# Two chained transformer blocks with routed experts: the order in which expert weights and first rows reach TensorE

## The chip, the cores and the metric

The kernel runs on one core of one Trainium2 chip. The metric is the device time of one execution in microseconds (us). Before the change the median of three runs is 1183.91 us (1180.22 to 1186.23).

## What is computed

Two transformer blocks follow each other on 256 tokens of width 1024, all in float32. The first has pooling and sparse attention, cross attention to a memory, and a mixture of 32 experts; the second has two attentions and a mixture of 64 experts with a shared one. The change touches only the two mixtures. Cut to what matters, the reference of an expert layer is:

```python
# first block: h has 256 rows, 32 experts, the best two of one group of eight
out = out + jnp.einsum('nef,efd->nd', silu(h @ w_gate[e]) * (h @ w_up[e]) * gates[e], w_down[e])
# second block: 64 experts, the best eight of four groups, weights summing to 2.5
g = jnp.sum(one_hot(eidx, 64) * w[..., None], axis=-2)
routed = sum over e of (silu(h @ w_eg[e]) * (h @ w_eu[e]) * g[:, e, None]) @ w_ed[e]
return routed + (silu(h @ w_sg) * (h @ w_su)) @ w_sd
```

An expert takes 1024 inputs to 256 hidden values and back, so its weights are 6 MB: 2 MB each of gate, up and down. The host packs them per expert into `w1_pack` and `w2_pack`, 128 partitions by 6144 columns: columns 0 to 2047 are gate and up for the first four chunks of the inputs (k = 0 to 3), columns 2048 to 4095 those for k = 4 to 7, and columns 4096 to 6143 are the down weights, ordered by output half (1024 columns for outputs 0 to 511, then 1024 for 512 to 1023).

## The kernel before

**Quads.** Only the rows that chose an expert are computed with it. They come in slabs of at most 32 rows, and four slabs make a quad: they stand in the four 32-wide lanes of one 128-row tile, each lane with its own expert. For one quad all four experts' weights are needed, 12 MB in each part of three: part g = 0 (k = 0 to 3, four lanes of 1024 KB), g = 1 (k = 4 to 7) and g = 2 (down), 4 MB a part. They live in `quad_w`, a view of the buffer `wring` by part and lane. Each part has one buffer, so it is loaded again when the quad before has used it. All weights are loaded by SP (SyncE) on one queue, in program order: for quad i it waits for `quad_gate_up_half` and loads part 0 for the next, for `quad_gate_up_made` and loads part 1, for `quad_down_made` and loads part 2 (L586 to L611 in the first block, L616 to L650 in the second). `load_lane` (L491) is one DMA of 1024 KB for a lane of part 0 or 1. `load_down` (L487) is one DMA of 512 KB for one output half of a lane; the callers issue half 1 of all four lanes and then half 0 of all four, and each half has its own semaphore.

PE (TensorE) does a quad in `quad` (L1041): the matmuls of part 0 and part 1 (L1066), eight transposes of the next quad's rows (`turn_rows`, L1037), two of the hidden values (L1077), then the down matmuls of half 1 (L1088), a mixing matmul that adds them to their tokens (L1097), and the same for half 0. It waits for the weights of a half by that half's semaphore:

```python
for half in (1, 0):
    ...
    pe.wait_ge(E(f"moe{n}_quad_down_loaded{half}"), i * 64)
```

The first block has eight quads. The first two are written out, with weights for the second in buffers that are free then (`second_gate_up`, `second_half`); only its parts of 1 for lanes 2 and 3 and its down weights go into `wring`. The rest is a loop over a register.

**Large items.** In the second block experts with more than 32 rows are done first, as tiles of up to 128 rows, two per pass of a loop (`items` of each engine). SP loads such an item's gate and up weights (2048 KB, L515) once PE has used the buffer, and its down weights (1024 KB, L525). Between the passes 1 and 2 (counted from 0) SP also loads parts of the first quad: `first_half` (L551) is part 1 for lanes 0 and 1, into `kmT_vm` and `tmp`. Lanes 2 and 3 of part 1 are loaded when the last item has freed `wring`. After the items come the quads; for this input there are five, and they gather the items' results meanwhile.

DVE (VectorE) prepares the first item: after the lists are made it runs `tile_shares` (L1986 to L2008: gate values per row, then the one-hot tiles for the quads' gates and the rows of the results), `quads_opened`, and then the scaling of the first item's rows out of PSUM (L2209), for which PE waits. POOL (GpSimd) gathers rows and stores results through its own DMA queue.

## Time and profile before

| | |
|---|---|
| Median of three runs | 1183.91 us |
| The profiled execution's own time | 1184.56 us |
| Its span in the trace | 1182.7 us |
| PE busy (matmul) | 991.0 us, 84% |
| DVE / ACT / POOL busy | 413.3 / 204.6 / 179.2 us |
| DMA moved | 382.71 MB, 324 GB/s on average |
| Mean granted PE clock | 0.925 of full |

The busy share of PE is an average over stages. The projections and attentions are PE's, with the DMA engines partly idle; the quads have the DMA engines full and PE waiting. So the table says where time is spent, and the chain of waits and the windows by stage say what each stage is bound by. The execution's own time is 1.86 us more than its span.

### The profile page before, as it was taken

The page shows a single profiled execution, that of the slowest core. Times are in us where ns is not written, and L with a number is a line of the kernel's source. Part 1 is how long each engine was busy: PE and PEld are TensorE (multiplying, and loading weights), DVE is VectorE, ACT ScalarE, POOL GpSimd, SP SyncE. Part 2 cuts the span into 40 slices and gives each one's busy share as a digit, 9 for nine tenths or more (in the row PEclk, how much of TensorE's full clock was granted, in tenths as well). Part 3 has the DMA queues.
Part 4 walks back from the last instruction along what each step waited for, and adds up shares of the span by engine and source line. Part 5 has one row for each costly group of instructions (what it writes and reads, how often), then busy time and mean ns, then how long its engine had stood idle before and what let it go on. Part 6 is the DMA issues. An engine that isn't in the chain of part 4 may idle for free.

```text
span 1182.7 us, 13815 instructions
## 1 busy us (share of the span) xinstructions
PE 991.0 (84%) x4939; PEld 531.1 (45%) x4939; DVE 413.3 (35%) x929; ACT 204.6 (17%) x439; POOL 179.2 (15%) x242
## 2 busy tenths in 40 slices
PE   6999998895786666689999998879999999965666
PEld 3545533342221111134556545468688787611111
DVE  1795212235100000024754123764323333145412
ACT  2204201311110101130533303101111111100000
POOL 1000010100000000000000000054455454133000
PEclk9999998896988878899999998889999999997788
DMA  8551567897989999973469886789999999999996
GB/s 316 209 213 72 197 243 314 305 365 307 407 345 417 417 417 416 419 235 130 170 257 343 327 334 246 322 330 417 364 358 362 367 363 351 356 414 416 414 417 274
DMA packets 79841, 382.71 MB, mean 324 GB/s; under 512 B 22008, under 2 KB 24308, under 8 KB 54523
## 3 DMA queue, kind: packets, MB, share of 16 engines
q1 hardware_dynamic: 64075, 330.64, 72.0%
q0 software_dynamic: 15728, 51.58, 11.5%
q8 instruction: 22, 0.36, 0.1%
q14 instruction: 16, 0.13, 0.0%
HBM read 347.05 MB, written 50.24 MB: 336 GB/s over the span
## 4 chain that ended last, share of the span: by engine, by line
PE 47%; DMA 21%; DVE 3%; SPq 2%; issue 1%; ACT 1%; DVEq 0%; POOLq 0%
DMA wring<-in_w_pack 21%; PE bank L887 16%; PE bank L1133 13%; PE bank L1145 6%; PE bank L1066 6%; PE bank L1088 1%; SPq L493 1%; PE bank L898 1%; PE bank L1097 1%; PE bank L952 1%; PE bank L919 1%; PE bank L1037 0%; SPq L489 0%; DMA kT<-xn_dram,token_now 0%; PE bank L926 0%
## 5 line engine op out<-in xcount | busy, mean ns | idle before, releaser
L887 PE MATMUL bank<-wring,hT 128*128 128x512 f32 (+3 forms) x608 | 249.7, 571 | 5.7 <-DVEq L1714 3.8
L1066 PE MATMUL bank<-wring,kT 128*32 128x512 f32 x768 | 118.1, 753 | 74.8 <-DMA wring<-in_w_pack 72.1
L887 PEld LDWEIGHTS bank<-wring,hT 128*128 128x128 f32 x608 | 114.0, 200 | 132.4 <-issue 122.5
L1133 PE MATMUL bank<-qT,wring 128*128 128x128 f32 x1408 | 163.0, 279 | 8.2 <-DVE qT L2209 5.6
L1133 PEld LDWEIGHTS bank<-qT,wring 128*128 128x128 f32 x1408 | 162.5, 196 | 13.1 <-DVE qT L2209 5.9
L1066 PEld LDWEIGHTS bank<-wring,kT 128*32 128x32 f32 x768 | 28.0, 134 | 157.5 <-DMA wring<-in_w_pack 88.3
L760 POOL DMA_INDIRECT PRT<-xn_parts_dram,part_now x88 | 89.7, 1019 | 40.0 <-issue 29.8
L1145 PE MATMUL bank<-wring,PRT 128*128 128x512 f32 x176 | 77.4, 592 | 0.0
L1097 PE MATMUL bank<-yT 128*128 128x512 f32 x104 | 55.2, 655 | 19.6 <-ACT yT L1534 5.7
L887 PE MATMUL bank<-wring,yT 128*128 128x512 f32 x160 | 71.0, 597 | 0.7 <-ACT yT L1440 0.7
L1088 PE MATMUL bank<-wring,kiT 128*32 128x512 f32 x416 | 55.4, 654 | 11.0 <-ACT kiT L1529 5.7
L2149 DVE TENSOR_TENSOR PRT<-bank,PRT 128x256 f32<-128x256 f32 x13 | 5.5, 423 | 163.5 <-ACT PRT L1527 163.5
L2231 DVE TENSOR_TENSOR PRT<-bank,PRT 128x256 f32<-128x256 f32 x22 | 9.3, 425 | 129.7 <-ACT PRT L1513 129.7
L1145 PEld LDWEIGHTS bank<-wring,PRT 128*128 128x128 f32 x176 | 32.6, 190 | 36.8 <-issue 36.8
L1440 ACT ACTIVATE wring<-bank 128x512 f32<-128x512 f32 (+3 forms) x40 | 21.8, 563 | 157.8 <-PE bank L887 156.1
L2221 DVE TENSOR_SCALAR qT<-yT,gs,modc 128x128 f32<-128x128 f32 x176 | 47.9, 347 | 0.8
L1527 ACT ACTIVATE PRT<-bank 128x256 f32<-128x256 f32 x13 | 5.0, 384 | 248.4 <-PE bank L1066 248.4
L887 PEld LDWEIGHTS bank<-wring,yT 128*128 128x128 f32 x160 | 29.7, 190 | 40.1 <-issue 39.0
L1097 PEld LDWEIGHTS bank<-yT 128*128 128x128 f32 x104 | 18.6, 199 | 59.1 <-ACT yT L1532 13.8
L734 POOL DMA_DIRECT2D wring<-in_w_ada x24 | 12.8, 532 | 211.7 <-PE bank L1179 73.5
L808 POOL COPY token_now<-token_list 128x1 uint32 (+1 forms) x15 | 4.0, 269 | 252.4 <-PE bank L1037 218.8
L855 POOL COPY kmT_vm<-tmp 128x1024 f32<-128x1024 f32 x2 | 2.1, 1040 | 255.4 <-DVEq L1714 255.4
(372 smaller groups left out, 1028.7 us busy)
## 6 DMA issues: line engine op xcount, KB each, us to landing
wring<-in_w_pack SPq DMA_DIRECT2D x118, 1024.0 KB, 16.5
wring<-in_w_pack SPq DMA_DIRECT2D x104, 512.0 KB, 17.8
wring<-in_w_pack SPq DMA_DIRECT2D x22, 2048.0 KB, 9.4
y_dram<-gateB SPq DMA_DIRECT2D x8, 4096.0 KB, 19.4
wring<-in_w_ada POOLq DMA_DIRECT2D x24, 1024.0 KB, 6.7
wring<-in_pack_z.0 SPq DMA_DIRECT2D x1, 2048.0 KB, 10.9
wring<-in_pack_z.2 SPq DMA_DIRECT2D x1, 2048.0 KB, 17.2
wring<-in_pack_z.3 SPq DMA_DIRECT2D x1, 2048.0 KB, 8.8
```

What stands on the lines that cost most here:

```text
L493: sp.dma_start(quad_w[:, g, j, :], A[f"w{n}_pack"][bass.ds(e, 1), :, 2048 * g:2048 * (g + 1)].rearrange("o p n -> p (o n)"))\
L734: pool.dma_start(w, A["w_ada_2"][0][k * P:(k + 1) * P, cols_]).then_inc(E(f"ada_loaded{q % ADA_BUFFERS}"), 16)
L760: pool.indirect_dma_start(xg[:, slot, 256 * g:256 * (g + 1)], None, xn_parts_dram, bass.IndirectOffsetOnAxis(ap=part_now[:, slot, g:g + 1] ...
L887: mm = nc.tensor.matmul(b[:, 0:n], lhs(k, t), w[:, k, c0:c0 + n], start=(k == 0), stop=(k == nk - 1))
L898: tr = nc.tensor.transpose(b[0:m, j * P:(j + 1) * P], piece, ident[:])
L1066: mm = nc.tensor.matmul(bank[lane[j], 0, :], xqT[:, k, lane[j]], w[:, (k % 4) * 512:(k % 4 + 1) * 512], start=(k == 0), stop=(k == KD - 1))
L1088: mm = nc.tensor.matmul(bank[lane[j], 2 + half, :], hidqT[:, f, lane[j]], quad_w[:, 2, j, c0:c0 + 512], start=(f == 0), stop=(f == 1))
L1097: mm = nc.tensor.matmul(bank[:, 4 + 2 * t + half, :], mix[:, t * P:(t + 1) * P], ysq[:, half, :], start=first, stop=False, skip_group_chec ...
L1133: mm = nc.tensor.matmul(bank[:, 2 + s, f * P:(f + 1) * P], item_gate_up(s)[:, k, f * P:(f + 1) * P], xT[:, s, k, :], start=(k == 0), stop= ...
L1145: mm = nc.tensor.matmul(bank[:, 4 * s + half, :], hidT[:, s, f, :], item_down(s)[:, half, f, :], start=(f == 0), stop=(f == 1))
L1440: drained(nc.scalar.activation(dst, src, func, scale=scale))
L2221: ins = V.tensor_scalar(xT[:, slot, k, :].rearrange("p (g w) -> p g w", g=4), blocks[:, k], gain[:, k:k + 1], shift[:, k:k + 1], ALU.mult, ...
```

## The change

- **First item's rows early.** `tile_shares` is cut in two. The first part (gate values) stays; the one-hot tiles and the result rows become `gate_tiles`, which DVE runs after the first pass of items. `quads_opened(2)` comes before `tile_shares`.
- **Whole down weights.** `load_down` loads a lane's down weights in one DMA of 1024 KB, with one semaphore for both halves, and PE waits for all four lanes before half 1. This holds for every quad but the last of each block.
- **Last four slabs in pieces.** The last quad of each block leaves the loop. SP loads its part 1 and part 2 by `load_last`, as pieces of 512 KB: k = 4, 5 of all lanes, then k = 6, 7, then down half 1, then half 0, each piece with its own semaphore. PE turns the next rows between part 0 and part 1 and waits in the middle of part 1. A third entry of `pairs_n` holds the number of the quad before the last, read into registers by PE and SP.
- **A third half lane.** Part 1 for lane 2 of the second block's first quad is loaded with the two others among the first large items, into `gateB[:, 0, :]` and `qiT`, as two DMAs of 512 KB. After the items SP loads the second quad's part 1 for lane 2 in its place.

The core of the diff:

```diff
-            def load_down(n, half, j, e):
-                c0 = 1024 * half
-                sp.dma_start(quad_w[:, 2, j, c0:c0 + 1024], A[f"w{n}_pack"][bass.ds(e, 1), :, 4096 + c0:5120 + c0].rearrange("o p n -> p (o n)"))\
-                    .then_inc(E(f"moe{n}_quad_down_loaded{half}"), 16)
+            def load_down(n, j, e):
+                sp.dma_start(quad_w[:, 2, j, :], A[f"w{n}_pack"][bass.ds(e, 1), :, 4096:6144].rearrange("o p n -> p (o n)"))\
+                    .then_inc(E(f"moe{n}_quad_down_loaded"), 16)
+
+            def load_last(n, g, experts):
+
+                for part in ((0, 1) if g == 1 else (1, 0)):
+                    c0 = 1024 * part
+                    for j, e in enumerate(experts):
+                        sp.dma_start(quad_w[:, g, j, c0:c0 + 1024], A[f"w{n}_pack"][bass.ds(e, 1), :, 2048 * g + c0:2048 * g + c0 + 1024].rearrange("o p n -> p (o n)"))\
+                            .then_inc(E(f"moe{n}_last_loaded{2 * g + part}"), 16)
...
-                for j in range(2):
+                for j in range(3):
                     e = sp.value_load(item_base[0:1, j:j + 1], min_val=0, max_val=E2 - 1)
-                    load_first_half(j, first_half[j], e)
+                    if j < 2:
+                        load_first_half(j, first_half[j], e)
+                    else:
+                        for part in range(2):
+                            sp.dma_start(third_half[part], A["w2_pack"][bass.ds(e, 1), :, 2048 + 1024 * part:3072 + 1024 * part].rearrange("o p n -> p (o n)"))\
+                                .then_inc(E("moe2_first_half_loaded"), 16)
...
-                with sp.Fori(3, quads_n) as i:
+                before_last = last_quad(sp, 1)
+                with sp.Fori(3, before_last) as i:
...
+                load_part(0, before_last, experts)
+                for g in (1, 2):
+                    sp.wait_ge(E(freed[g]), before_last)
+                    load_last(1, g, experts)
...
-                for j in (2, 3):
-                    load_first_half(j, quad_w[:, 1, j, :], first[j])
+                load_lane(2, 1, 2, second[2])
+                load_first_half(3, quad_w[:, 1, 3, :], first[3])
...
-                load_quad(1, second, (range(4), (2, 3)))
+                load_quad(1, second, (range(4), (3,)))
...
+                        if g == 1 and last is not None:
+                            pe.wait_ge(E(f"moe{n}_quad_result_copied"), i)
+                            turn_rows(i * 16 + 16)
...
+                        elif g == 1 and last is not None:
+                            pe.wait_ge(E(f"moe{n}_last_loaded2"), 64)
...
+                            if k == 6 and last is not None:
+                                pe.wait_ge(E(f"moe{n}_last_loaded3"), 64)
...
-                        pe.wait_ge(E(f"moe{n}_quad_down_loaded{half}"), i * 64)
+                        if last is not None:
+                            pe.wait_ge(E(f"moe{n}_last_loaded{4 + half}"), 64)
+                        else:
+                            pe.wait_ge(E(f"moe{n}_quad_down_loaded"), i * 64)
...
                 pairs = pair_count(dve)
+                quads_opened(2)
+
                 tile_shares()
-                quads_opened(2)
...
                 pair_of(0)
+                gate_tiles()
                 gates_taken()
```

The order of DVE at the first item. Before (`kT` and `share` are the gate values, `kmT_vm` and `y_rows` the one-hot tiles and result rows, `qT<-bank` the rows that PE waits for):

```order
L1995 TENSOR_REDUCE share<-kT 128x16
L1996 TENSOR_SCALAR st<-st 128x16
L2000 TENSOR_TENSOR kmT_vm<-lists,st 128x136
L2001 TENSOR_TENSOR kmT_vm<-kmT_vm,share 128x136
L2000 TENSOR_TENSOR kmT_vm<-lists,st 128x136
L2001 TENSOR_TENSOR kmT_vm<-kmT_vm,share 128x136
L2004 TENSOR_SCALAR st<-st 128x16
L2005 TENSOR_TENSOR share<-share,st 128x16
L2006 TENSOR_TENSOR st<-st 128x16
L2007 TENSOR_SCALAR st<-st 128x16
L2008 TENSOR_TENSOR y_rows<-st 128x16
L2209 TENSOR_SCALAR qT<-bank,gs,modc 128x128 x8
```

With the change, at the same place:

```order
L2044 TENSOR_REDUCE share<-kT 128x16
L2264 TENSOR_SCALAR qT<-bank,gs,modc 128x128 x8
L2271 STREAM_TRANSPOSE yT<-PRT 128x1024
L2276 TENSOR_SCALAR qT<-yT,gs,modc 128x128 x8
L2286 TENSOR_TENSOR PRT<-bank,PRT 128x256
```

Ten instructions now stand behind the first pass of items, and the rows follow the reduction.

The order of SP in the first block, from the first quad's extra buffers to the loop. Before (`wring<-in_w_pack 128x1024` is a half of a lane's down weights, 128x2048 a whole lane of a part):

```order
L493 DMA wring<-in_w_pack 128x2048 x4
L598 DMA wring<-in_w_pack 128x2048 x2
L493 DMA wring<-in_w_pack 128x2048 x2
L489 DMA wring<-in_w_pack 128x1024 x8
L493 DMA wring<-in_w_pack 128x2048 x2
L489 DMA wring<-in_w_pack 128x1024 x8
L448 TENSOR_LOAD pairs_n
```

With the change:

```order
L506 DMA wring<-in_w_pack 128x2048 x4
L613 DMA wring<-in_w_pack 128x2048 x2
L506 DMA wring<-in_w_pack 128x2048 x2
L494 DMA wring<-in_w_pack 128x2048 x4
L506 DMA wring<-in_w_pack 128x2048 x2
L494 DMA wring<-in_w_pack 128x2048 x4
L449 TENSOR_LOAD pairs_n
L454 TENSOR_LOAD pairs_n
```

The bytes and their order by part are the same; eight half transfers have become four whole ones at both places, and a second register load follows.

The order of SP among the first large items, with the change (`kmT_vm` and `tmp` are the lanes 0 and 1 as before, `gateB` and `qiT` the added lane 2, and the 128x4096 transfer behind them is the next pass's first item):

```order
L568 DMA kmT_vm<-in_w_pack 128x2048
L556 TENSOR_LOAD item_base
L556 ISA x2
L568 ISA
L568 DMA tmp<-in_w_pack 128x2048
L556 TENSOR_LOAD item_base
L556 ISA x2
L561 ISA
L561 DMA gateB<-in_w_pack 128x1024
L561 ISA
L561 DMA qiT<-in_w_pack 128x1024
```

The two last transfers are new here; the loop over the passes follows them on the same queue.

## Rows read from the trace of the kernel before

**Rows 1.** The page, parts 2 and 4: rate per slice, shares of the chain

```profile
GB/s 316 209 213 72 197 243 314 305 365 307 407 345 417 417 417 416 419 235 130 170 257 343 327 334 246 322 330 417 364 358 362 367 363 351 356 414 416 414 417 274
...
PE 47%; DMA 21%; DVE 3%; SPq 2%; issue 1%; ACT 1%; DVEq 0%; POOLq 0%
```

**Rows 2.** Chain that ended last, second quad of the first block (start, us, what)

```profile
307.77 16.45 DMA wring<-in_w_pack
...
324.36 3.67 PE bank L1088 x16
...
332.49 2.27 PE bank L1088 x16
334.77 0.33 SPq L489
```

**Rows 3.** Windows there (length; busy time and instructions per engine; PE clock; DMA share; GB/s)

```profile
331.00:338.00 7.00, 6.27 (x30) 1.41 (x32) 0.40 (x2) 1.88 (x2) 0.00 (x0) 0.84 0.47 154
338.00:346.00 8.00, 7.82 (x70) 2.75 (x62) 1.32 (x4) 0.53 (x2) 0.19 (x1) 1.00 1.01 363
```

**Rows 4.** Windows in the first block, later: down weights, then gate and up weights

```profile
431.50:441.50 10.00, 8.02 (x44) 2.45 (x44) 1.26 (x3) 0.77 (x2) 0.18 (x1) 0.66 1.03 413
441.50:462.50 21.00, 11.38 (x72) 3.12 (x72) 1.23 (x4) 2.48 (x3) 1.02 (x1) 1.00 1.01 419
```

**Rows 5.** Timeline of PE, first block (start, us, what, idle before and its releaser)

```profile
370.68 5.34 PE L1066 MATMUL bank<-wring,kT 128*32 128x512 f32 x32 [4.75 <-DMA wring<-in_w_pack]
...
377.89 1.93 PE L1088 MATMUL bank<-wring,kiT 128*32 128x512 f32 x16 [0.47 <-ACT kiT L1529]
...
433.00 6.60 PE L1066 MATMUL bank<-wring,kT 128*32 128x512 f32 x32 [3.48 <-DMA wring<-in_w_pack]
...
453.90 3.64 PE L1066 MATMUL bank<-wring,kT 128*32 128x512 f32 x32 [3.23 <-DMA wring<-in_w_pack]
```

**Rows 6.** Chain, last quad of the first block

```profile
494.07 5.09 PE bank L1066 x32
...
505.67 1.90 PE bank L1088 x16
```

**Rows 7.** Chain, first large items of the second block

```profile
776.89 0.19 DVE st L1996
...
779.95 2.65 DVE qT L2209 x8
...
799.35 6.87 PE bank L1145 x16
...
818.61 15.68 DMA wring<-in_w_pack
```

**Rows 8.** Windows: first items; the other items; the quads after them

```profile
778.00:834.30 56.30, 49.13 (x328) 41.13 (x328) 25.73 (x74) 5.88 (x12) 26.92 (x36) 0.94 1.02 412
850.50:1019.80 169.30, 169.30 (x1154) 138.69 (x1153) 60.27 (x160) 23.53 (x48) 81.73 (x105) 1.00 0.95 358
1026.00:1160.00 134.00, 82.99 (x490) 24.64 (x488) 45.87 (x76) 4.16 (x10) 25.57 (x27) 0.82 1.02 412
```

**Rows 9.** Timeline: a result store of POOL, then the wait of PE

```profile
830.94 1.03 POOL L772 DMA_INDIRECT y_dram<-PRT,row_now  x1 [0.87 <-POOL row_now L767]
...
834.32 5.91 PE L1133 MATMUL bank<-qT,wring 128*128 128x128 f32 x36 [2.55 <-DMA wring<-in_w_pack]
```

**Rows 10.** Chain, last quad of the second block

```profile
1162.35 5.34 PE bank L1066 x32
...
1169.57 1.97 PE bank L1088 x16
...
1174.29 1.90 PE bank L1088 x16
```

**Rows 11.** Windows at the end of the last weights

```profile
1171.00:1172.00 1.00, 0.49 (x8) 0.00 (x0) 0.83 (x3) 0.00 (x0) 0.00 (x0) 1.00 0.12 49
1172.00:1173.00 1.00, 0.70 (x2) 0.46 (x3) 0.25 (x1) 0.00 (x0) 0.00 (x0) 1.00 0.00 0
```

More of the change, by code:

```diff
@@ L445, in quad_count, with last_quad @@
         def quad_count(engine, n):
-            least = FIXED_QUADS if n == 1 else 3
+            least = FIXED_QUADS if n == 1 else 4
             return engine.value_load(pairs_n[0:1, 1:2], min_val=least, max_val=QUADS[n])
+        def last_quad(engine, n):
+            least = FIXED_QUADS if n == 1 else 4
+            return engine.value_load(pairs_n[0:1, 2:3], min_val=least - 1, max_val=QUADS[n] - 1)
         def item_gate_up(s):
@@ L534, in items @@
                     if j >= 2:
-                        for half in (1, 0):
-                            load_down(2, half, j, e)
+                        load_down(2, j, e)
                 load_pair(1, True)
@@ L562, in first_quad @@
                 sp.wait_ge(E("ada_steps_made"), ADA_GROUPS * ADA_STEPS)
-                for half in (1, 0):
-                    for j in range(4):
-                        load_down(1, half, j, j)
+                for j in range(4):
+                    load_down(1, j, j)
                 sp.wait_ge(E("xn_ready"), 6)
@@ L586, in load_part @@
                     sp.wait_ge(E(freed[g]), made)
-                    for half in (1, 0) if g == 2 else (None,):
-                        for j in lanes:
-                            if g == 2:
-                                load_down(1, half, j, experts[j])
-                            else:
-                                load_lane(1, g, j, experts[j])
+                    for j in lanes:
+                        if g == 2:
+                            load_down(1, j, experts[j])
+                        else:
+                            load_lane(1, g, j, experts[j])
                 second, third = range(4, 8), range(8, 12)
@@ L624, in lane_after @@
                     else:
-                        for half in (1, 0):
-                            load_down(2, half, j, experts[j])
+                        load_down(2, j, experts[j])
                 first, second = quad_experts(0), quad_experts(1)
@@ L1038, in turn_rows, with quad @@
                     tr.then_inc(E(f"moe{n}_quad_rows_turned"), 1)
-                def quad(i, first):
-                    second = n == 1 and not first and isinstance(i, int)
+                def quad(i, first, last=None):
+                    second = n == 1 and not first and last is None and isinstance(i, int)
                     pe.wait_ge(E(f"moe{n}_quad_rows_copied"), i)
                     for g in range(2):
+                        if g == 1 and last is not None:
+                            pe.wait_ge(E(f"moe{n}_quad_result_copied"), i)
+                            turn_rows(i * 16 + 16)
                         if g == 0 and second:
@@ L1047, in quad @@
                         elif g == 0 and n == 1 and not first:
[L1048 removed]
+                            pe.wait_ge(E("moe1_quad_loaded0"), i * 64 - 64 if last is None else last * 64)
                         elif g == 1 and second:
@@ L1111, in quads @@
                 quads_n = quad_count(pe, n)
-                with pe.Fori(3 if n == 1 else 2, quads_n + 1) as i:
+                with pe.Fori(3 if n == 1 else 2, quads_n) as i:
                     quad(i, False)
+                quad(quads_n, False, last_quad(pe, n))
             def items():
@@ L1995, in tile_shares, with gate_tiles @@
                 link(V.tensor_reduce(share, same, X, ALU.add))
+            def gate_tiles():
+                k_n, q_n = TAKES[2], QUADS[2] + 1
+                row, item = [st[:, c:c + 16].rearrange("p (t k) -> p t k", t=2) for c in (326, 342)]
                 link(V.tensor_scalar(item, item, float(WHOLE), None, ALU.subtract))
@@ L2090, in quad_experts @@
                 link(V.tensor_scalar(whole, whole, float(FIXED_QUADS), None, ALU.add))
+                V.tensor_scalar(pairs_n[0:1, 2:3], whole, 1.0, None, ALU.subtract)
                 link(V.tensor_copy(pairs_n[0:1, 1:2], whole))
```

45 lines of the change are left out of this document (32 added, 13 removed).

## The prediction

> **What bounds the kernel now.** I read the page first for the rate of the DMA engines per slice and the shares of the chain [rows 1]. In three stretches the rate stands at 414 to 419 GB/s: slices 13 to 17, 36 to 39 and one around slice 28. 21% of the chain is the expert weights' DMA. So the quads of both blocks are bound by bytes, and there a change of order moves the end only if it changes the bytes in the stretch, lets the queue run dry, or changes what PE does behind the last transfer. Next I read windows by stage [rows 8]: the first items (778 to 834 us) run at 412 GB/s with a DMA share of 1.02, full too; the other items at 358 GB/s with PE busy all the time, so PE bounds them; the quads after them at 412 GB/s, full. Then the chain, for what each stretch waits on, and the timeline for PE within a quad.
>
> The transfers land in the order of their issue. A window of 10 us behind a part 1's landing moves at 413 GB/s and the 21 us behind it at 419 [rows 4]: 10 us is a part's 4 MB, so the first holds the half down transfers (512 KB) and the second the whole lanes (1024 KB). At 416 GB/s 2 MB take 5.0 us and 1 MB 2.5 us. I use this as a ruler for landings.
>
> **Part by part.** Signs: plus is slower.
>
> *Whole down weights, second quad of the first block: +4.5.* PE starts half 1 at 324.36, released by a DMA issued at 307.77; that is half 1 of all four lanes [rows 2]. Half 0 lands 5.0 us behind it by the ruler. With whole lanes PE needs both, so it starts at 329.4. From there to the release of SP takes 10.4 us (324.36 to 334.77), with the matmuls of half 1 at the lower clock already (3.67 us there [rows 2], 1.93 in [rows 5]). SP issues the third quad's down weights only then, and the queue runs dry meanwhile: 154 GB/s between 331 and 338 [rows 3]. The 5.0 us add to that drought, and all that follows in this block is FIFO behind it. Against it: between 338 and 346 the rate is only 363 GB/s [rows 3], 1.0 us of 8 lost, which with four issues in place of eight may go. Ends: +5.5 and, if the dip goes and the restart is quicker, +3.4. I take 4.5.
>
> *Whole down weights elsewhere in the first block: -0.6.* In the later quads PE wants half 1 at 377.89 [rows 5], 7.2 us behind part 1's landing at 370.7, and the whole part lands 10.1 us behind it. So PE waits 2.9 us more per quad, but the queue then still holds 8 MB (20 us) of the next parts, so it does not run dry and the wait is hidden; its cover is that queue. The rate of 413 becomes 419 for 4 MB: 0.15 us a quad, five quads, 0.75 us; the last quad's part 1 in pieces gives 0.15 back. Bounds: 0 and -1.5.
>
> At this place the Trainium skill speaks. The row shows that halving a transfer costs 1.4% of its rate while the queue is full [rows 4]. The Trainium skill, page "DMA: Bandwidth & Descriptors", sections "Anatomy of one DMA" and "Bandwidth", says a DMA takes some 2.0 us and its bytes at 436 GB/s, and to batch to at least 1 MiB. By that, as an estimate, eight halves cost 8 us more than four wholes, and the sum would be some 45 us faster. The trace does not bear it out: transfers overlap.
>
> *The last quad of the first block in pieces: -1.5.* Part 1 lands at 494.07 (call it T), PE starts down half 0 at 505.67, T + 11.6 [rows 6]. With pieces only k = 6, 7 is left at T: 1.8 us at the full clock (half of 3.64), 3.4 at the lower (half of 6.6) [rows 5], then 1.9 us to half 1 as in [rows 10] (1162.35 + 5.34 to 1169.57). That would give T + 5.3 at the latest; half 1 lands at T + 5.0 and half 0 at T + 10.1. So the weights behind it take over, and half 0 starts at T + 10.1. Bounds 0 and -2.6. The turned rows were beside the hidden values' path before, so moving them gives nothing.
>
> *First rows early and the third half, among the first items: 0 and +2.5.* DVE's ten instructions take 776.89 to 779.95, 3.1 us, on the chain [rows 7]; PE could start 3.1 us earlier. But PE waits 2.55 us until 834.32 for a DMA issued at 818.61 [rows 7, 9], and the stretch before it is full [rows 8]. Bytes ahead of that transfer decide when it lands, not PE. So the 3.1 us become a longer wait: worth 0. The third half puts 1 MB ahead of the same transfer: +2.5. Behind it PE is the bound, with the engines at 358 of 412 GB/s, so this passes whole to the end. `gate_tiles` moves to behind the first pass, where PE does 6.9 us of down matmuls (from 799.35 [rows 7]) before it needs them; 3 us are hidden there. Ends: -3.1 if the early rows pay fully and the megabyte is hidden, up to +5.0 if the result stores of the second pass (two of 512 KB, the first issued at 830.94 [rows 9]), now 3 us earlier, all go ahead too. The Trainium skill, same page, section "Queues, rings and completion order", says each DMA engine takes turns between the queues; no row here shows the turns themselves.
>
> *The quads of the second block: -2.9.* The stretch from 1026 to 1160 is full [rows 8]. It has 1 MB less (lane 2's part 1 of the first quad): -2.5. Three and a half quads' down weights whole, less part 1 in pieces: -0.4. In the fourth quad PE waits some 3 us more for half 1, under the queue again.
>
> *The last quad of the second block: -1.9.* T is 1162.35; half 0 starts at 1174.29, T + 11.9 [rows 10]. The last bytes pass between 1171 and 1172 and none after [rows 11]: T + 10 with the landing. So half 0 starts 1.9 us earlier. Bounds 0 and -3.4.
>
> *Small ones: +0.2.* One DVE instruction on the path to the second lists. The added register loads of PE and SP lie in front of waits for DMA.
>
> **Sum.** 4.5 - 0.6 - 1.5 + 2.5 - 2.9 - 1.9 + 0.2 = +0.3. Against the profiled execution (1184.56: the span of 1182.7 and 1.86 around it) this is 1184.9. The median is 0.65 below that execution, so I predict **1184.2** for the median. About 0.5% (5.9 us) is what a measurement of this kernel can tell from no change.
>
> **The rivals.**
>
> *The early rows pay (chance 0.21).* If the stretch from 778 is not as full as its share says, the 3.1 us arrive and the megabyte is hidden. For: the share is of engines busy, not of bytes at the best rate, 412 of 419. Against: PE waits at its end for a transfer issued 15.7 us earlier. Time: 1184.2 - 2.5 - 3.1 = 1178.6. With the tails at their better ends it is below 1178.
>
> *The pieces do not pay (0.13).* The 16 DMA engines end out of step, and each piece is in only when the slowest is. If half 0 lands at T + 11.6 or later in both blocks, both tails give 0: 1184.2 + 3.4 = 1187.6, and 1190 with the larger toll among the items. For it: the share falls off over several us at the end.
>
> *PE's clock (0.09), slower.* The chip grants PE 1.2 instead of 2.4 GHz behind idle stretches: a part's 32 matmuls take 6.60 or 3.64 us [rows 5]. The whole down weights put a third wait into each quad. If that keeps the clock at the lower level throughout, a quad is 13.2 us for two parts, up to 3.8 for transposes and hidden values (twice the 1.9), 10.4 from half 1 to SP's release [rows 2] and 3.7 for the last mixing (it takes as long as half 1): 31.1 us. Its bytes take 31.2 (370.68 to 433.00 is two quads [rows 5]). From there each further us of waiting in a quad goes to the end. At 1 us in each of eight such quads, and with no gain in the tails, it is 1184.2 + 8 + 3.4 = 1195.6. Against: the queue holds 20 us.
>
> *The number of transfers counts (0.02).* If each DMA had its issue, 0.43 us, in series, four fewer in ten quads less eight more in two would give -14: 1170. The rate of 413 against 419 speaks against it.
>
> *The change does less than it says* is not a rival here: the printed orders show each move.
>
> **The numbers.** Forecast as summed: 0.55, its own range 1180.5 to 1188.5. The range over all cases, 1177.5 to 1190, leaves out the clock case, the transfer count and the faster end of the first rival, some 0.2. Over 0.5% faster (below 1178): 0.4 of the early rows' 0.21, 0.02 of the count, and 0.05 of the rest: 0.15. Over 0.5% slower: 0.09, a third of the pieces' 0.13, and 0.05 from the forecast with its upper ends: 0.18. Within: 0.67.
>
> **What would show each step.** Down half 1 of the first block's second quad starts near 329, and the windows behind it are dry for 5 us longer. Later quads keep their 31 us distance. In both last quads down half 0 starts 10 us behind the last piece of part 1. PE's first item starts 3 us earlier by the clock of its own stretch, and the wait of the third pass (number 2) grows from 2.5 us to 8. From its end to the start of the quads nothing changes; from there to the last weight there are 2.9 us less. A third pass without a longer wait, or a second quad's half 1 without its 5 us, would prove the sum wrong.

## The result, and the profile after

The changed kernel takes **1185.80 us** (median of 20 runs) against 1181.12 us of the kernel before beside it (20 runs). The ratio is 1.0038, 95% interval 1.0024 to 1.0052: 4.5 us slower (2.8 to 6.2). The ratio's centre is within 0.5% and the median inside the forecast range, but the sum had +0.3 us. The profiled execution took 1191.89 us, near the upper end of its runs, so stages are read below from more than one trace. One run of e2 below, of 3474.34 us, is left out of its median and ratio.

One size given above needs a correction: 6144 columns of float32 on 128 partitions are 3 MB, so an expert's weights are 3 MB, 1 MB each of gate, up and down, and a quad's 12 MB are its three parts of 4 MB together. The argument uses the 4 MB.

I cut each trace into three stages by PE's timeline. *Front* runs from down half 1 of block 1's first quad to down half 0 of its last, *middle* from there to the first quad of block 2, *quads* from there to the end of the span. Before they are 205.7, 522.3 and 154.8 us; after 207.1, 525.7 and 157.3.

**Front.** Windows of the changed kernel at the place of [rows 3] (length; busy time and instructions per engine; PE clock; DMA share; GB/s):

```profile
331.00:338.00 7.00, 6.29 (x24) 1.59 (x20) 0.00 (x0) 0.60 (x1) 0.00 (x0) 0.60 0.11 46
338.00:346.00 8.00, 7.28 (x56) 2.13 (x52) 0.77 (x3) 1.88 (x2) 0.00 (x0) 1.00 0.78 296
```

The queue is dry for longer, as forecast: 46 in place of 154 GB/s, then 296 in place of 363. Against 416 GB/s these 15 us lose 8.5 us of transfer; before they lost 5.4. SP issues the third quad's down weights at 338.77:

```profile
338.77 1.98 SPq L494 DMA_DIRECT2D wring<-in_w_pack  x4
```

[Rows 2] have 334.77 there. The end of block 1, PE's timeline (start, us, what, idle before and its releaser):

```profile
492.16 1.92 PE L1109 MATMUL bank<-wring,kT 128*32 128x512 f32 x16
495.71 1.92 PE L1109 MATMUL bank<-wring,kT 128*32 128x512 f32 x16 [1.63 <-DMA wring<-in_w_pack]
...
500.94 3.37 PE L1135 MATMUL bank<-wring,kiT 128*32 128x512 f32 x16 [1.90 <-DMA wring<-in_w_pack]
505.02 1.98 PE L1144 MATMUL bank<-yT 128*128 128x512 f32 x4 [0.71 <-ACT yT L1580]
506.94 1.92 PE L1135 MATMUL bank<-wring,kiT 128*32 128x512 f32 x16
```

T, the landing of the last piece of part 1, is 495.71 (494.07 in [rows 6]). Half 1 comes at T + 5.2 as forecast; half 0 at T + 11.2, where I had T + 10.1. There is no wait ahead of half 0: its last piece had landed at T + 10.2 (505.89, by its semaphore), and PE was still at work. Its down half 1 ran mostly at the lower clock (3.37 us in place of 1.92), and with the mixing matmuls behind it PE takes 6.0 us from half 1 to half 0.

**Middle.** The first item passes of the changed kernel, same view:

```profile
781.40 17.31 PE L1181 MATMUL bank<-qT,wring 128*128 128x128 f32 x128 [2.82 <-DVE qT L2264]
...
812.15 17.30 PE L1181 MATMUL bank<-qT,wring 128*128 128x128 f32 x128 [1.27 <-DMA wring<-in_w_pack]
829.29 7.03 PE L1193 MATMUL bank<-wring,PRT 128*128 128x512 f32 x16
838.85 15.96 PE L1181 MATMUL bank<-qT,wring 128*128 128x128 f32 x128 [2.53 <-DMA wring<-in_w_pack]
```

The third pass starts 4.5 us later than in [rows 9] (3.2 us by the clock of its own stage), with the same wait ahead of it, not 8 us; the second pass has a wait that was not there before. The first pass starts 2.6 us earlier in its stage, close to the forecast 3.

**Quads of block 2.** What PE waited for from 1030 to 1165 us in the changed kernel (total us, times, longest):

```profile
PE bank L1070 <- DMA kT<-xn_dram,token_now: 40.6, 2, 23.7
...
PE bank L1109 <- DMA wring<-in_w_pack: 1.9, 3, 0.9
```

And the same view of the kernel before, from 1026 to 1160 us:

```profile
PE bank L1066 <- DMA wring<-in_w_pack: 22.1, 4, 8.9
PE bank L1037 <- DMA kT<-xn_dram,token_now: 12.6, 2, 10.4
```

This was in none of my terms. Before, PE waited mostly for weights; now it waits for the rows of the next quad, a gather on POOL's queue. The two waits together were 34.7 us and are 42.5. Windows of the changed kernel, the whole stretch and a hole in it:

```profile
1030.00:1160.00 130.00, 76.66 (x468) 24.97 (x470) 45.99 (x76) 4.15 (x10) 24.73 (x27) 0.79 0.96 391
```

```profile
1094.00:1096.00 2.00, 2.00 (x17) 0.42 (x16) 0.00 (x0) 0.00 (x0) 0.00 (x0) 0.90 0.51 213
1096.00:1098.00 2.00, 1.18 (x6) 0.49 (x3) 1.59 (x2) 0.00 (x0) 0.00 (x0) 1.00 0.49 76
```

391 GB/s in place of the 412 of [rows 8]: a stretch that was always full runs dry, because PE, late behind its rows, frees the lanes late. POOL's timeline of the changed kernel shows the gathers ahead of the rows:

```profile
1055.79 0.99 POOL L836 DMA_INDIRECT PRT<-y_dram,y_rows  x1 [5.79 <-DVE hT L2306]
1059.54 0.98 POOL L836 DMA_INDIRECT PRT<-y_dram,y_rows  x1 [2.76 <-DVE hT L2306]
1063.28 0.99 POOL L836 DMA_INDIRECT PRT<-y_dram,y_rows  x1 [2.76 <-DVE hT L2306]
1067.04 0.99 POOL L836 DMA_INDIRECT PRT<-y_dram,y_rows  x1 [2.76 <-DVE hT L2306]
1068.03 0.19 POOL L841 COPY token_now<-token_list 128x1 uint32<-128x1 uint32 x1
1069.06 1.86 POOL L845 DMA_INDIRECT kT<-xn_dram,token_now  x1 [0.84 <-issue]
```

Each result gather needs the buffer that DVE frees when an earlier one has landed and been added. They stand 3.75 us apart. The row gather for the third quad waits in line behind them; PE has its rows at 1082.61. The chain that ended last begins at such a gather:

```profile
1103.62 16.19 DMA PRT<-y_dram,y_rows
```

The end of the block, from the same chain and from PE's timeline: PE waits for the last piece, which lands at 1181.3.

```profile
1164.52 16.78 DMA wring<-in_w_pack
```

```profile
1181.44 1.92 PE L1135 MATMUL bank<-wring,kiT 128*32 128x512 f32 x16 [1.57 <-DMA wring<-in_w_pack]
```

### The profile page after: what moved, and what is told of

It reads as the page before. It is cut to its first block and busy times, and to the rows that moved or that the text cites. A ratio compares the mean times of both kernels' runs of the same rounds, so it can differ in the third digit from the quotient of the medians.

```text
span 1190.0 us, 13739 instructions
## 1 busy us (share of the span) xinstructions
PE 993.4 (83%) x4939; PEld 537.7 (45%) x4939; DVE 413.5 (35%) x931; ACT 204.4 (17%) x439; POOL 177.7 (15%) x242
## 3 DMA queue, kind: packets, MB, share of 16 engines
q0 software_dynamic: 15728, 51.58, 11.5%
## 5 line engine op out<-in xcount | busy, mean ns | idle before, releaser
L1181 PE MATMUL bank<-qT,wring 128*128 128x128 f32 x1408 | 166.2, 282 | 6.6 <-DMA wring<-in_w_pack 3.8
L1181 PEld LDWEIGHTS bank<-qT,wring 128*128 128x128 f32 x1408 | 165.6, 199 | 11.7 <-DMA wring<-in_w_pack 4.9
L1109 PE MATMUL bank<-wring,kT 128*32 128x512 f32 x760 | 104.0, 674 | 36.7 <-DMA wring<-in_w_pack 34.1
L1135 PE MATMUL bank<-wring,kiT 128*32 128x512 f32 x416 | 59.2, 693 | 32.4 <-DMA wring<-in_w_pack 30.0
L1144 PE MATMUL bank<-yT 128*128 128x512 f32 x104 | 60.5, 710 | 19.5 <-ACT yT L1582 5.8
L1109 PEld LDWEIGHTS bank<-wring,kT 128*32 128x32 f32 x760 | 25.9, 121 | 105.7 <-issue 59.7
L1070 PE MATMUL bank<-ident,kT 128*128 128x128 f32 x112 | 17.9, 311 | 45.8 <-DMA kT<-xn_dram,token_now 45.8
L1193 PEld LDWEIGHTS bank<-wring,PRT 128*128 128x128 f32 x176 | 32.4, 190 | 38.4 <-issue 33.5
L1135 PEld LDWEIGHTS bank<-wring,kiT 128*32 128x32 f32 x416 | 12.5, 119 | 68.3 <-issue 64.4
## 6 DMA issues: line engine op xcount, KB each, us to landing
wring<-in_pack_z.0 SPq DMA_DIRECT2D x1, 2048.0 KB, 10.3
```

Of the source, the lines that this page charges most:

```text
L1070: tr = nc.tensor.transpose(bank[:, 1 + k // 4, (k % 4) * P:(k % 4 + 1) * P], xq[:, k * P:(k + 1) * P], ident[:])
L1109: mm = nc.tensor.matmul(bank[lane[j], 0, :], xqT[:, k, lane[j]], w[:, c0:c0 + 512], start=(k == 0), stop=(k == KD - 1))
L1135: mm = nc.tensor.matmul(bank[lane[j], 2 + half, :], hidqT[:, f, lane[j]], quad_w[:, 2, j, c0:c0 + 512], start=(f == 0), stop=(f == 1))
L1144: mm = nc.tensor.matmul(bank[:, 4 + 2 * t + half, :], mix[:, t * P:(t + 1) * P], ysq[:, half, :], start=first, stop=False, skip_group_chec ...
L1181: mm = nc.tensor.matmul(bank[:, 2 + s, f * P:(f + 1) * P], item_gate_up(s)[:, k, f * P:(f + 1) * P], xT[:, s, k, :], start=(k == 0), stop= ...
L1193: mm = nc.tensor.matmul(bank[:, 4 * s + half, :], hidT[:, s, f, :], item_down(s)[:, half, f, :], start=(f == 0), stop=(f == 1))
```

## The experiments

Theory: a ledger of bytes, as in the prediction. Rival C, formed on the trace above: whole down weights hold up the gathers of POOL's queue. Each kernel was timed beside the kernel before. "Us" below is the ratio's difference from 1 times 1182. An interval of a single ratio is about 1.5 to 2 us to either side, and that of a difference between two rows about 3 us, so of single differences only the larger ones are certain.

| kernel | median us | ratio (95%) | us | front, middle, quads |
|---|---|---|---|---|
| e1 early rows alone | 1180.94 | 0.9993 (0.9974 to 1.0012) | -0.8 | 207.4, 520.5, 155.2 |
| e2 third half alone | 1183.97 | 1.0014 (1.0002 to 1.0027) | +1.7 | 205.5, 525.6, 152.1 |
| e3 pieces alone | 1181.00 | 0.9989 (0.9977 to 1.0002) | -1.3 | 203.5, 520.4, 153.9 |
| e4 pieces and whole down weights | 1183.14 | 1.0015 (0.9999 to 1.0030) | +1.8 | 206.3, 520.8, 154.9 |
| e5 the change again | 1187.35 | 1.0041 (1.0025 to 1.0057) | +4.8 | 207.4, 525.3, 156.0 |
| e6 change, block 2 in halves | 1185.28 | 1.0019 (1.0000 to 1.0038) | +2.2 | 206.9, 524.2, 153.3 |
| e7 change, block 2 in 2 KB runs | 1188.78 | 1.0059 (1.0036 to 1.0082) | +7.0 | 207.2, 525.2, 155.9 |
| e8 change, second quad in halves | 1183.26 | 1.0011 (0.9992 to 1.0029) | +1.3 | 201.0, 524.7, 154.4 |
| e9 e6 and e8 together | 1178.62 | 0.9978 (0.9960 to 0.9995) | -2.6 | 201.4, 522.9, 153.1 |
| e10 before, lanes later | 1180.84 | 0.9983 (0.9968 to 0.9998) | -2.0 | 207.6, 518.3, 156.0 |
| e11 e9, lanes later | 1176.30 | 0.9964 (0.9945 to 0.9982) | -4.3 | 200.8, 522.4, 152.2 |
| e12 e11, block 1 in halves too | 1181.27 | 0.9992 (0.9974 to 1.0010) | -0.9 | 202.9, 524.6, 153.6 |

### One part at a time

**e1.** The early rows alone:

```diff
                 pairs = pair_count(dve)
+                quads_opened(2)
+
                 tile_shares()
-                quads_opened(2)
...
                 pair_of(0)
+                gate_tiles()
                 gates_taken()
```

> The kernel before with only the first item's rows made early (the rest of the shares' work moved behind the first pass). My theory (bytes set the first items): the first item starts 1 to 3 us earlier, the wait ahead of the third pass grows by as much, 0.0 us in the time (within 1 us). Rival A (the early rows pay): 2 to 3 us faster. Rival B (the moved work now stands behind the first pass, on DVE's way to the second): up to 2 us slower.

-0.8 us, not told from zero. PE's timeline of e1 shows where the time goes:

```profile
780.86 17.30 PE L1133 MATMUL bank<-qT,wring 128*128 128x128 f32 x128 [2.81 <-DVE qT L2214]
...
811.69 17.25 PE L1133 MATMUL bank<-qT,wring 128*128 128x128 f32 x128 [2.26 <-DMA wring<-in_w_pack]
...
835.65 14.45 PE L1133 MATMUL bank<-qT,wring 128*128 128x128 f32 x128
```

The wait comes at the second pass, not the third, and goes from the third. The pass behind it costs more too: the windows of e1 show a granted clock of 0.50, the lower level, from 811.7 to 817,

```profile
811.70:817.00 5.30, 5.30 (x25) 5.30 (x26) 4.00 (x11) 0.00 (x0) 2.31 (x3) 0.50 1.00 422
```

so the second pass takes 17.25 us. It took 14.46 before, where PE ran through. The wait isn't shown to be the whole reason: in e3, e4 and e10 no wait stands ahead of the second pass, and it takes 15.96 to 15.98 us, at the lower level for a shorter time. Timeline and a window of e3:

```profile
806.90 15.96 PE L1178 MATMUL bank<-qT,wring 128*128 128x128 f32 x128
```

```profile
808.00:810.00 2.00, 2.00 (x11) 2.00 (x11) 2.00 (x7) 0.00 (x0) 0.00 (x0) 0.50 1.00 422
```

So a second pass is 1.5 us slower without any wait, and how much of the 2.8 us is the wait's isn't shown. In return the third pass, without its wait, takes 14.45 us in place of 16.19.

**e2.** The third half alone:

```diff
-                for j in range(2):
+                for j in range(3):
...
-                for j in (2, 3):
-                    load_first_half(j, quad_w[:, 1, j, :], first[j])
+                load_lane(2, 1, 2, second[2])
+                load_first_half(3, quad_w[:, 1, 3, :], first[3])
```

> The kernel before with only the third half lane loaded among the large items. My theory (a ledger of bytes): the third pass waits 2.5 us longer, the start of the quads is 2.5 us later, and the quads get it back with 1 MB less, the last weight lands 0 us later: 0.0 us (within 1 us). Rival C (the small quads of block 2 are bound by the row gathers on POOL's queue and not by bytes alone, so that they give nothing back): 2.5 us slower.

The third pass waits

```profile
836.76 16.86 PE L1142 MATMUL bank<-qT,wring 128*128 128x128 f32 x128 [5.19 <-DMA wring<-in_w_pack]
```

5.19 us in place of 2.55, 2.6 more: the ruler was right. The quads take 152.1 in place of 154.8 us, 2.7 less: right too. But the middle loses 3.3 us against the trace of before, so the two do not cancel: 0.6 us by these stages, +1.7 us by the runs. The 3.3 are 2.6 of longer wait and 0.7 of a slower pass behind it (16.86 us against 16.19); from the end of that pass to the quads both traces take 177.4 us. Against e3 and e4 the middle loses 5 us, because their third pass waits only 0.97 and 1.17 us, behind the slower second pass, and then takes 14.56 us.

**e3, e4.** e4 is the change without early rows and third half. e3 is e4 with the down weights in halves outside the last quads, and so the kernel before with the pieces alone. e3 against e4:

```diff
-            def load_down(n, j, e):
+            def load_down(n, half, j, e):
+                c0 = 1024 * half
...
-                    for j, e in enumerate(experts):
-                        load_down(2, j, e)
+                    for half in (1, 0):
+                        for j, e in enumerate(experts):
+                            load_down(2, half, j, e)
...
-                            pe.wait_ge(E(f"moe{n}_quad_down_loaded"), i * 64)
+                            pe.wait_ge(E(f"moe{n}_quad_down_loaded{half}"), i * 64)
```

> The kernel before with only the last four slabs of each block in pieces, the down weights everywhere else in halves as before. My theory: 3.4 us faster (1.5 in block 1, 1.9 in block 2), half 0 starting 10 us behind the last piece a of part 1. As the trace of the full change has half 0 at 11.2 and 11.6 us behind the landing of piece b, a rival (pieces don't pay) says 0 to 1 us faster only.

> As e3_pieces, and with the down weights whole in all quads but the last of each block. My theory, as measured in the trace of the full change: against e3 +2.3 us in the second quad of block 1, -1 us in the later ones, so +1.3 us, and nothing in block 2. Rival C (whole down weights hold up the row gathers of POOL's queue in block 2, PE waits on rows): 4 us or more slower than e3, with PE idle behind the row gathers of the second, third and fourth quads of block 2 by 17 us or more each.

Pieces alone give -1.3 us, not -3.4. The whole down weights cost 3.1 us on top (e4 against e3). In e4 PE's idle time ahead of the row turns of block 2 is 36.7 us; in e3, e1 and e2 it is 13.4, 13.7 and 21.0 (the third half in e2 adds some 8 us to that wait and takes them from the wait for weights, 13.0 us there). With e4, which has neither early rows nor third half, the cause of the slow gathers is the whole down weights. By the stages of the two traces, though, e4 loses 2.8 us to e3 in the front and only 1.0 in the quads. The waits of 17 us or more came in two quads, not three.

### Where whole down weights cost

**e5.** 

> The changed kernel itself once more, beside the next three. Theory C (the whole down weights slow the gathers on POOL's queue in block 2): PE idle ahead of the row turns of block 2's quads is again 35 us or more (12.6 in the trace of before), the result gathers behind the first four stand 3.7 us apart (2.9 in before), time 3 to 5 us above before. Rival (the first trace of the change was a disturbed one): idle near 20, gathers near 2.9 us apart.

PE's idle time ahead of the turns is 40.6 us again, and the gathers stand 3.7 to 3.8 us apart. This profiled execution is near the upper end of its runs too (1190.4 us), but e4 and e8, whose profiled ones are among their faster half, show the same: 36.7 and 41.1 us. The first trace was not an exception.

**e6.** Block 2 in halves again, by a `load_half` beside `load_down`, at its three places, with PE waiting for each half by itself; one of the places:

```diff
-                    for j, e in enumerate(experts):
-                        load_down(2, j, e)
+                    for half in (1, 0):
+                        for j, e in enumerate(experts):
+                            load_half(half, j, e)
```

> The change with the down weights of block 2 in halves again (block 1's stay whole). Theory C: gathers 2.7 us apart, PE idle ahead of the row turns near 20 us as in e2_third, 2 us faster than the change. Rival (only the bytes count in block 2, and the toll is in block 1): the same time as the change, within 1 us.

2.6 us faster than e5 by the ratios, which alone is not told from zero, and the quads take 153.3 in place of 156.0 us. The same step from e8 to e9, below, is 3.9 us and 1.3 in the quads; the two together are clear of zero. What PE waited for in e6, 1030 to 1160 us:

```profile
PE bank L1078 <- DMA kT<-xn_dram,token_now: 21.6, 2, 16.8
PE bank L1117 <- DMA wring<-in_w_pack: 16.9, 6, 6.3
```

**e7.** As many DMAs as in halves, but smaller runs; PE's wait counts the eight of them:

```diff
             def load_down(n, j, e):
+                if n == 2:
+                    dst = quad_w[:, 2, j, :].rearrange("p (h b n) -> p h b n", h=2, b=2)
+                    src = A["w2_pack"][bass.ds(e, 1), :, 4096:6144].rearrange("o p (h b n) -> p (o h) b n", h=2, b=2)
+                    for b in range(2):
+                        sp.dma_start(dst[:, :, b, :], src[:, :, b, :]).then_inc(E("moe2_quad_down_loaded"), 16)
+                    return
```

> The change with each down lane of block 2 loaded by two DMAs of 512 KB, as many as in halves, but each made of 2 KB runs (every other 512 columns) in place of 4 or 8 KB; PE still waits for both. Theory C1 (a gather gives way to one packet of the weights at each turn, so the packet's size sets its latency): gathers 2.5 us apart or less, idle ahead of the turns 20 us or less, provided the weights' own rate holds. Theory C2 (the number of DMAs, or how far ahead SP's queue is filled, sets it): gathers as in halves, 2.7 us. If small packets cost rate (below 400 GB/s in 1050 to 1090 us), it is slower than the change for that.

POOL's timeline of e7:

```profile
1057.35 0.99 POOL L842 DMA_INDIRECT PRT<-y_dram,y_rows  x1 [5.71 <-DVE hT L2312]
1059.38 0.99 POOL L842 DMA_INDIRECT PRT<-y_dram,y_rows  x1 [1.04 <-DVE hT L2312]
1061.41 0.99 POOL L842 DMA_INDIRECT PRT<-y_dram,y_rows  x1 [1.04 <-DVE hT L2312]
```

and of e6, the same gathers:

```profile
1053.89 0.99 POOL L844 DMA_INDIRECT PRT<-y_dram,y_rows  x1 [5.52 <-DVE hT L2316]
1056.30 0.99 POOL L844 DMA_INDIRECT PRT<-y_dram,y_rows  x1 [1.42 <-DVE hT L2316]
1058.87 0.99 POOL L844 DMA_INDIRECT PRT<-y_dram,y_rows  x1 [1.57 <-DVE hT L2316]
```

The gathers stand 2.03 us apart beside 2 KB runs, about 2.5 beside 4 KB and 3.75 beside 8 KB, at the same number of DMAs in the first two. So between those two the size of the run decides, theory C1, and not the number of DMAs. Over the seven intervals from the fifth result gather to the twelfth it is 16.4 us (e7), 18.1 to 20.4 (the nine kernels whose block 2 is in halves, before among them) and 25.9 to 27.6 (e4, e5, e8 and the change). Yet e7 has the highest median of all, not told apart from e5's: its windows from 1055 to 1115 move 404 and 406 GB/s, those of e6 414 and 414. Also PE waits for both parts of the down weights, 12.0 us in four waits.

```profile
1055.00:1085.00 30.00, 14.26 (x90) 4.83 (x86) 17.24 (x23) 0.77 (x2) 9.48 (x10) 0.72 1.04 404
1085.00:1115.00 30.00, 14.26 (x94) 4.16 (x86) 16.99 (x23) 0.77 (x2) 7.85 (x8) 0.79 1.03 406
```

The Trainium skill, page "DMA: Bandwidth & Descriptors", section "Queues, rings and completion order", says that a DMA engine takes its queues in turn and changes only between packets. The runs agree. The DMA queues of the changed kernel (1056 to 1064 us), of e6 (1058 to 1066) and of e7 (1062 to 1070), where both queues have work all the time; q1 is SP's, q0 POOL's (packets, MB, share of 16 engines):

```profile
q1 hardware_dynamic: 310, 2.24, 67.5%
q0 software_dynamic: 300, 1.06, 33.3%
```

```profile
q1 hardware_dynamic: 464, 1.70, 53.1%
q0 software_dynamic: 433, 1.57, 49.0%
```

```profile
q0 software_dynamic: 571, 2.01, 63.9%
q1 hardware_dynamic: 605, 1.17, 38.7%
```

The two queues pass nearly the same number of packets, whatever their size: one of the weights for one of the rows (77 to 113 of the packets of each window are under 512 bytes and carry neither). A gather's row is 4 KB, so 1.06, 1.57 and 2.01 MB are 259, 383 and 491 rows in 8 us, or one gather of 128 rows in 4.0, 2.7 and 2.1 us (an estimate), close to the distances of 3.75, 2.5 and 2.03. I had cited that rule ahead of the result and not drawn this from it.

**e8.** The second quad of block 1 in halves, again with PE waiting for each half by itself:

```diff
-                load_part(2, 1, second)
+                sp.wait_ge(E(freed[2]), 1)
+                for half in (1, 0):
+                    for j in range(4):
+                        c0 = 1024 * half
+                        sp.dma_start(quad_w[:, 2, j, c0:c0 + 1024], A["w1_pack"][4 + j, :, 4096 + c0:5120 + c0]).then_inc(E(f"moe1_second_down_loaded{half}"), 16)
```

> The change with the down weights of block 1's second quad alone in halves again. My theory (the toll at the front is what the stream of block 1 passes on): half 1 starts 4.4 us earlier in its quad, SP's release of the third quad's down weights likewise, and the last part 1 of block 1 lands 2.3 us earlier: 2 to 3 us faster than the change. Rival: the queue's reserve takes it up and it is 0 to 0.5 us.

3.5 us faster than e5, the front 6.4 us shorter. The windows of e8 where the queue ran dry:

```profile
331.00:338.00 7.00, 6.75 (x52) 2.22 (x56) 0.77 (x3) 1.49 (x2) 0.00 (x0) 1.00 0.96 360
338.00:346.00 8.00, 4.81 (x46) 1.99 (x42) 1.71 (x3) 0.77 (x2) 1.19 (x2) 1.00 1.02 425
```

The drought is gone, more fully than in the kernel before: the granted clock is 1.00 there against 0.84 in [rows 3]. In this profile PE was back at the upper of its two levels (2.4 GHz) by 326 us, in that of before by about 333. The early return is in e3, e8, e9, e11 and e12, the late one in before, e1, e2 and e10 (26.5 to 27 us behind the first quad's half 1 against 33 to 33.5); half 1 starts 23.0 to 23.7 us behind the first quad's in the former and 24.3 to 24.5 in the latter. All that have pieces, and halves here, are early, all without pieces late, though the pieces are used 160 us later. Why I can't say. It is worth some 3 us in this stage of a trace. So 6.4 us is too high as the price of the whole weights. The 3.5 of the runs is the better figure, but it holds whatever the early return gives as well; and e3's -1.3 us may be this rather than its tails.

**e9.** 

> The change with halves both in block 1's second quad and in all of block 2: early rows, third half and pieces stay, and whole down weights only in block 1's later quads. If the two costs add (3.5 us for the second quad by e8, 2.5 us for block 2 by e6), it is 6.0 us faster than the change, 1181 us or 1.2 us below before. If they are one cost seen twice (a toll at the front that only comes out in block 2), it is 3.5 us faster than the change.

7.4 us faster than e5 (0.9978 against 1.0041), 2.6 below before. The costs add, as far as some 3 us of uncertainty tell: one cost seen twice would have been 3.5 us, which is outside.

### The transfer that the third pass waits for

**e10.** The kernel before, with one line more ahead of its two half lanes:

```diff
+                load_pair(2, True)
                 sp.wait_ge(E("moe2_experts_listed"), 1)
                 for j in range(2):
...
-                with sp.Fori(2, pairs) as i:
+                with sp.Fori(3, pairs) as i:
```

> The kernel before with its two half lanes of 1 MB (first quad of block 2) issued behind the weights of the third pass in place of ahead of them. My theory (bytes ahead of the third pass's transfer set it): the third pass's wait of 2.55 us goes, the later passes hide the 2 MB beside PE, 2.5 us faster. Rival (the transfer that is moved then delays the fourth pass by as much): 0 us, with the wait at the fourth pass.

-2.0 us. The third pass starts without a wait,

```profile
831.97 14.45 PE L1134 MATMUL bank<-qT,wring 128*128 128x128 f32 x128
```

and the fourth too: from here PE runs through. Bytes ahead of that transfer did set the wait.

**e11.** The same line in e9, with three half lanes behind it.

> e9 with all three half lanes behind the third pass's weights. My theory: the third half's 3.3 us among the first passes go with the 2.5 us wait of before, while the quads keep their 2.7 us: 5 us faster than e9, 1176 us, 0.5% faster than before. Rival (the fourth pass waits for the 3 MB): within 1 us of e9.

1176.30 us, 4.3 us below before (2.1 to 6.5) and the fastest median here. But against e9 it is 1.7 us, not 5, which is not told from zero. The third pass has no wait, the fourth has one:

```profile
852.28 14.56 PE L1198 MATMUL bank<-qT,wring 128*128 128x128 f32 x128 [1.60 <-DMA wring<-in_w_pack]
```

The truth lies between theory and rival: 3 MB behind the third pass's weights, with PE early by the early rows, are more than the fourth pass can wait out; e10's 2 MB were not.

**e12.** `load_down` in halves everywhere, else as e11.

> e11 with halves in block 1's later quads too: of the change's whole down weights nothing is left, while early rows, third half, pieces and the later lanes stay. It tells what whole down weights are worth where they have cover. My term for them was -0.6 us (0 to -1.5), so this should be 0.6 us slower than e11, or 1177 us (0.5% below before); a rival (fewer, larger DMAs leave the queue earlier and PE's clock in another state) would make it 2 us or more slower; equal or faster would say that the whole weights bring nothing anywhere.

0.9992 against 0.9964: 3.3 us slower than e11, with some 3 us of uncertainty. The front shows the same sign: 202.9 and 203.5 us in the kernels with halves and an early clock (e12, e3), 200.8 to 201.4 with whole weights in the later quads (e11, e8, e9). But only part of it comes from the weights' own flow: the landing T of the last part 1 stands 191.5 and 191.8 us behind the stage's start in e3 and e12, and 190.5 to 191.1 in e8, e9 and e11, 0.9 us on average. The rest stands behind T: PE starts half 0 at T + 12.0 and 11.1 in the former and at T + 10.3 in the latter, because there half 1 ran at the upper clock. That isn't a matter of whole weights, as the changed kernel, e5, e6 and e7 have them and start at T + 11.2 to 11.3. PE's timeline of e8:

```profile
494.90 1.92 PE L1141 MATMUL bank<-wring,kiT 128*32 128x512 f32 x16 [0.47 <-ACT kiT L1583]
...
499.73 1.92 PE L1141 MATMUL bank<-wring,kiT 128*32 128x512 f32 x16 [0.20 <-DMA wring<-in_w_pack]
```

So whole down weights are worth about 1 us by the traces in block 1's later quads (3.3 by the runs, with their 3 of uncertainty); there the queue covers PE's wait and nothing else is seen to share the DMA engines.

## Why the prediction was right, and where not

The range held the time, but the sum was +0.3 us and the kernel is 4.5 us slower. That the median (1185.80) is only 1.6 us from the forecast 1184.2 is partly luck: the forecast stood on three runs of the kernel before, and beside the change that kernel measured 1181.12, not 1183.91. Some terms missed in opposite directions, too. By its steps:

- **Second quad of block 1, +4.5 (3.4 to 5.5).** Right. Half 1 started at 328.80 (forecast 329.4), SP's release moved by 4.0 us, and the runs give 3.5 us (e8 against e5; some 3 us of uncertainty, and the clock's early return is in it).
- **Whole down weights elsewhere in block 1, -0.6 (0 to -1.5).** Right: about -1 us by T, inside its bounds, though a little too small. The windows of the changed kernel from 431.5 to 462.5 move 422 and 420 GB/s in place of [rows 4]'s 413 and 419, which is 0.27 us a quad where I had taken 0.15. e12 against e11 has -3.3 us, with some 3 us of uncertainty.
- **Pieces, -1.5 and -1.9.** Too large. Together they gave -1.3 us (e3), and half 0 starts at T + 11.2 in block 1 and T + 11.6 in block 2 (T 1169.85, half 0 1181.44) in the changed kernel, where it was T + 11.5 (11.6 by the chain of [rows 6]) and T + 11.9. In block 1 the ruler was right, since the last piece lands at T + 10.2. The term left out PE's own way from half 1 to half 0: 4.6 us where half 1 runs at the upper clock (as in the kernel before), 6.0 here, behind a wait of 1.90 us. So half 1 came 1.7 us earlier and half 0 only 0.3. In block 2 the last piece itself is late. It lands at T + 11.5, 2.5 us behind the piece before it, where the others stand 1.3 apart; the kernel moves 238 GB/s from 1178 to 1180 us and 8 in the two behind. In the change, e5, e7 and e8 it lands at T + 11.3 to 11.5, in the others that show it at T + 10.0 to 10.2, as forecast. The second rival asked for T + 11.6 in both blocks: block 2 met that and block 1, where PE and not a landing set it, did not.
- **Early rows, 0.** Close: -0.8 us (e1). The reason needs a correction: the wait moves to the second pass, which is 2.8 us slower, and the third pass runs 1.7 us faster without one.
- **Third half, +2.5 there and -2.5 in the quads.** Both sizes hold at the places I named (5.19 us of wait; 2.7 us less in the quads), but PE's lower clock behind the longer wait adds 0.7 us. Net +1.7 us (e2).
- **Quads of block 2, -2.9. This is the step that failed.** Its sign was wrong, while the pieces were only too large. In e2, which loads halves, they give -2.7. With whole weights they take 156.0 and 157.3 us in place of 154.8. I had written that in the fourth quad "PE waits some 3 us more for half 1, under the queue again", and took the whole stretch to be bound by the weights' bytes. The gathers of POOL's queue share the DMA engines there. Beside 8 KB runs each takes 1.2 us longer, they follow one another, the rows come late, PE frees the lanes late, and the queue runs dry. By e6 against e5 that is 2.6 us, by e9 against e8 3.9; the quads' stage alone has 2.7 and 1.3, and 1.0 in e4 against e3.

With the terms as the runs have them, and the -0.9 of T for the later quads, +3.5 - 0.9 - 1.3 - 0.8 + 1.7 + 2.6 = +4.8 us, against the 4.5 measured. Each term has 1.5 to 3 us of uncertainty, so the agreement shows only that no large term is missing.

Two slips in the working change nothing. The transfers do not land strictly in the order of their issue: 11 of the kernel before's weight transfers land ahead of the one issued before them, by 1.2 us at most. And the estimate of 45 us does not fit the count of the transfers' rival: at 8 us for every four fewer, 32 fewer give 64.

What stays open: why the last piece of block 2 lands over 1 us late in four kernels, and what brings PE's clock back early in the second quad in five (all of them have pieces, and halves in that quad). A kernel with e11's loads but without early rows and third half, for which e10 speaks (its middle is the shortest), was not tried.

## What to carry to other kernels

A larger DMA was some 1 us better over five quads here, by the traces, where only the queue it stands in used the DMA engines. Where another queue's small transfers are on the path, the larger run made each of them wait longer; look for such a chain before merging, and merge where there is none. Here halves in two places and whole weights in the third beat both kernels.

A merged wait cost nothing that these traces show while the queue held work, and 3.5 of its 5.0 us where PE's release refilled an empty queue. Price each place for itself: the same edit was worth about +3.5, -1 and +2.6 us in three places.

## What the runs showed of the hardware

- A chain of gathers stands 2.03, about 2.5 and 3.75 us apart beside weight transfers with runs of 2, 4 and 8 KB on another queue, at nearly equal rates (404 to 417 GB/s). While both queues have work, they pass nearly equal numbers of packets (310 and 300, 464 and 433, 605 and 571 in 8 us), whatever the size of either's.
- A pass of 128 matmuls takes 14.45 us where PE keeps its upper clock level. It took 15.96 to 15.98 us with some 3 us at the lower level (0.50 granted) and no wait ahead of it (e3, e4, e10), and 17.25 us with about 5 us at that level behind a wait of 2.26 us (e1).
- The last 4 MB of a block landed 10.0 to 10.2 us behind the weights before them in every trace of block 1 that shows it, and in most of block 2, with or without pieces ahead of them. PE began on them up to 2.9 us later than that, by its own path.
- PE's clock in block 1's second quad came back to its upper level 6 to 7 us earlier in five kernels than in four others with the same loads there, and the stage was some 3 us shorter.
